# Feed-forward, first matrix: seven block products for a tile and its gate instead of eight

## The chip, the core and the metric

One core of one Trainium2 chip. The metric is the device time of one execution of the whole program in microseconds, the median of several runs. The engines are named as in the profile: PE (TensorE; PEld are its weight loads), DVE (VectorE), ACT (ScalarE), POOL (GpSimd), SP (SyncE, which here only issues transfers).

## The reference

One inference step of a decoder trunk of two layers, width 1024, for 512 prompt tokens and 8 x 4 sample tokens, 544 in all. Each layer has two half feed-forwards, one ahead of its mixers and one behind them; so the program has four feed-forward stages, and they are what the change touches:

```
x += 0.5 * gate * ((silu(a) * b) @ w_out),   a, b = split(mod(rmsnorm(x)) @ w_in, 2)
```

`w_in` is 1024 x 5632, `w_out` 2816 x 1024; `mod` multiplies by (1 + scale) and adds shift. Scale, shift and gate come from the conditioning of each sequence through a large matrix `ada_w` (adaLN); its product is cut into 36 units of 512 columns, 2 MB each, of which 32 are computed inside feed-forward stages (14, 6, 12 and 0 in the four). All is float32.

## The kernel before

The state `x` stays in SBUF, channels on partitions: 8 chunks of 128 channels by 544 tokens. A product in float32 precision is made of three in `fp32r`: each weight tile and each activation is split into a high part (an ACT copy, `split_hi`, L187) and a low part, the remainder (a DVE subtraction, `split_lo`, L192), and hi x hi, hi x lo and lo x hi are summed in PSUM. `some` (L204) issues the six matmuls of one chunk of 128 rows: three terms by two halves of 272 tokens.

A weight tile is 1024 x 128. There are two slots of raw, high and low tiles (`Weights`); SP loads a tile in three pieces (`load`, L175) as soon as the remainder of the tile that had the slot is made; ACT copies it when it has landed and the product that used the slot's high part is done; DVE makes the remainder; PE multiplies.

`ffn_stage` has 22 pairs of tiles (a tile of a and its gate tile of b) in three parts of 8, 8 and 6 pairs (`FFN_PARTS`). In each part the pairs are multiplied, then follow 8 output tiles, whose products run over the part's 8 or 6 chunks and are added to `x` by `residual` (L681 to L686). A pair is 96 matmuls: 8 chunks x 3 terms x 2 halves for `pa`, as many for `pg`. ACT applies Silu to `pa` (L748), DVE multiplies with `pg` (L790), ACT and DVE split the result into `ghi` (L752) and `glo` (L794). At the start of a stage `norm_vector` and `norm_scalar` make the normalised activations `nhi` and `nlo` chunk by chunk (L242 scales on DVE, L270 adds the shift on ACT and gives the high part, L247 the remainder), and `first_products` follows them chunk by chunk for the first pair.

Where a stage has units, one stands ahead of each pair's products: `ada_columns` (L419) and `ada_turn` (L432) on PE, `ada_copy` (L428) on ACT, `ada_add` (L441) on DVE, with two buffers for the 2 MB of a unit; `ada_load` (L410) refills them from ACT's queue.

GpSimd computes only in the HGRN2 stage (L1793, L1794). The order on every engine is written out by hand and held together by semaphores.

Of the kernel before, what the change touches and what calls it, by code (L numbers as in the profile page):

```python
# [27 lines left out]
P = 128  # L28
D, DEPTH, D_FF = 1024, 2, 2816
# [111 lines left out]
class Weights:  # L141
# [41 lines left out]
    def split_hi(self, act, where, k):  # L183
        u, slot = where
        act.wait_ge(self.raw_full[slot], 16 * PIECES * u + 16 * PIECES)
        act.wait_ge(self.mm_done, 2 * u + (slot + 1))
        act.activation(self.hi[slot][:, 0:k, :], self.raw[slot][:, 0:k, :], ACT.Copy).then_inc(self.hi_done, 1)  # L187

    def split_lo(self, dve, where, k):
        u, slot = where  # L190
        dve.wait_ge(self.hi_done, 2 * u + (slot + 1))
        dve.tensor_tensor(self.lo[slot][:, 0:k, :], self.raw[slot][:, 0:k, :],  # L192
                          self.hi[slot][:, 0:k, :].bitcast(F32), ALU.subtract).then_inc(self.lo_done, 1)
# [167 lines left out]
def trunk(nc, a, o):  # L361
    ctx = ExitStack()
    with ctx:
# [324 lines left out]
        def ffn_stage(l, which, w3, follow):  # L688

            names = NormSems.NAMES + RootSems.NAMES + AdaSems.NAMES + ("silu_done", "prod_done", "gh_done", "gl_done", "res_done", "x_done")  # L690
            with stage(nc, *names) as sems, ExitStack() as st:
                s, root, ada = NormSems(sems[0:5]), RootSems(sems[5:11]), AdaSems(sems[11:18])
                silu_done, prod_done, gh_done, gl_done, res_done, x_done = sems[18:]
                units = ADA_IN_FFN[l, which]
                if units:
                    ada_raw = [sb(f"ada_raw{i}", [P, DC, UNIT], at=st) for i in range(2)]
                    md = sb("md", [P, 2, P], at=st)
                nhi, nlo = (sb(n, [P, DC, T], F32R, at=st) for n in ("nhi", "nlo"))
                ghi, glo = (sb(n, [P, KMAX, T], F32R, at=st) for n in ("ghi", "glo"))
                tmp, ts = norm_buffers(st)  # L700
                sq = sb("sq", [P, 2, T], at=st)
                sa, g32 = sq, tmp
                rt = sb("rt", [P, 2, NSMP], at=st)
                pa = [ps(f"pa{i}", 2, st) for i in range(2)]
                pg = [ps(f"pg{i}", 2, st) for i in range(2)]
                block = st.enter_context(nc.Block())
                w_in = a["ffn_w_in"][l, which]
                w_out = a["ffn_w_out"][l, which]

                parts = []  # L710
                t = j0 = 0
                for n in FFN_PARTS:
                    after = DC if len(parts) + 1 < len(FFN_PARTS) or follow else None
                    parts.append((n, j0, t, t + 2 * n, after))
                    t, j0 = t + 2 * n + DC, j0 + n

                @block.sync
                def _(sp):
                    for n, j0, ti, to, _ in parts:
                        first = 1 if j0 == 0 else 0  # L720
                        for j in range(first, n):
                            for q in range(2):
                                c = (j + j0) * P + q * D_FF
                                wt.load(sp, wt.at(ti + q, j), wt.columns(DC, w_in[:, c:c + P]))
                            if j0 + j == 1:
                                for i in range(min(2, len(units))):
                                    ada_load(sp, ada, ada_raw, i, *units[i])
                        rows = w_out[j0 * P:(j0 + n) * P, :]
                        for c in range(DC):
                            wt.load(sp, wt.at(to + c), wt.columns(n, rows[:, c * P:(c + 1) * P]))  # L730
                    for q, tile in enumerate(follow):
                        wt.load(sp, wt.at(t + q), tile)

                @block.scalar
                def _(act):
                    norm_scalar(act, s, tmp, ts, mods, w3, nhi)
                    for n, j0, ti, to, after in parts:
                        def pair(j, last):
                            for q in range(2):
                                i = j0 + j + q - 1  # L740
                                if 0 <= i < len(units):
                                    ada_copy(act, ada, pg[q][:, 0, HALF:], md, i)
                                    if i + 2 < len(units):
                                        ada_load(act, ada, ada_raw, i + 2, *units[i + 2])
                                k = n if last and q == 1 else DC
                                wt.split_hi(act, wt.at(ti + 2 * q + 2, j), k)
                                act.wait_ge(prod_done, j + (j0 + q + 1))
                                act.activation(strided(sa[:, q, :], [HALF, 2], [1, HALF]), pa[q][:, :, 0:HALF],  # L748
                                               ACT.Silu).then_inc(silu_done, 1)
                                wt.split_hi(act, wt.at(ti + 2 * q + 3, j), k)  # L750
                                act.wait_ge(prod_done, j + (j0 + q + 3))
                                act.activation(ghi[:, bass.ds(j + q, 1), :], g32[:, q, :].unsqueeze(1), ACT.Copy).then_inc(gh_done, 1)  # L752

                        def chunks(c, last):
                            for q in range(2):
                                if not last:
                                    wt.split_hi(act, wt.at(to + q + 2, c), n)
                                elif after:
                                    wt.split_hi(act, wt.at(to + q + 2, c), after)

                        for j in range(0, n, 2):
                            pair(j, j == n - 2)
                        if j0 + n < D_FF // P:
                            for c in range(DC // 2):
                                chunks(c, c == DC // 2 - 1)
                            continue
                        for c in range(DC):
                            if c + 2 < DC or after:
                                wt.split_hi(act, wt.at(to + c + 2), n if c + 2 < DC else after)
                            act.wait_ge(res_done, DC * (len(parts) - 1) + c + 3)  # L770
                            square(act, root, x, c, sq)
# [3 lines left out]
                def _(dve):  # L775
                    dve.sem_inc(prod_done, 2)
                    dve.sem_inc(res_done, 2)
                    norm_vector(dve, s, x, rs, tmp, ts, mods, w3, nhi, nlo)
                    for c0, (n, j0, ti, to, after) in enumerate(parts):
                        def pair(j, last):  # L780
                            for q in range(2):
                                i = j0 + j + q - 2
                                if 0 <= i < len(units):
                                    ada_add(dve, ada, pg[q][:, 1, HALF:], units, i)
# [1423 lines left out]
```

## Time and profile before

| what | value |
|---|---|
| time, median of 3 runs (range) | 3281.62 us (3279.41 to 3281.9) |
| the profiled execution | 3281.45 us, span 3279.7 us |
| busy: PE, PEld, DVE, ACT, POOL | 92%, 87%, 41%, 29%, 2% of the span |
| PE instructions | 24911 |
| mean granted clock of TensorE | 0.941 |
| bytes read from HBM, written | 344.10 MB, 39.07 MB |

Rows of the profile that group instructions give line, engine, operation, output<-inputs with partitions x elements, count | busy us, mean ns of one | idle time of the engine just before them and what ended it. Rows of a timeline give start us, duration us, engine, line, operation, with the idle time before it and its releaser in brackets; "x2" merges two instructions. A start time counts from the beginning of the span.

### The profile page before, as it was taken

Reading aid. Unit: us, or ns where it says so; the run is one execution under the profiler, and the core shown is the slowest. Engines: PE = TensorE matmul, PEld = TensorE weight load, DVE = VectorE, ACT = ScalarE, POOL = GpSimd, SP = SyncE. Lnnn points to the kernel's source line nnn. Section 1 sums busy time; section 2 is a strip of 40 time slices with the busy share of each in tenths; the row PEclk is TensorE's granted clock in tenths of the full one; section 3 lists DMA queues with packets and bytes.
Section 4 is the critical chain, followed back from the end, with each engine's and each line's share of the span. In section 5 each row is a group of like instructions: output and inputs, shape, how many; then the busy total and the mean of one; then the engine's idle time right before and its main releaser. Section 6 shows DMA issues by size and latency. Waiting matters only on the chain. (4 is left out here: it accounts for less than half of the span.)

```text
span 3279.7 us, 58783 instructions
## 1 busy us (share of the span) xinstructions
PE 3015.7 (92%) x24911; PEld 2855.5 (87%) x24911; DVE 1347.5 (41%) x2793; ACT 964.3 (29%) x1594; POOL 57.4 (2%) x32
## 2 busy tenths in 40 slices
PE   6999998989679898999989999888985998899997
PEld 4999998878469898999989999887873998899997
DVE  3332334356355454333343333443553635433334
ACT  2222222344243233222232222332443413322222
POOL 0000000000030000000000000000000300000000
PEclk7999999899889899999989999989997998899998
DMA  6746224431542335332256522263215425232331
GB/s 201 248 133 205 85 81 148 99 116 53 116 123 79 112 114 194 107 90 85 83 176 202 159 84 87 88 177 99 65 51 150 100 70 158 65 90 85 91 89 62
DMA packets 523703, 378.65 MB, mean 115 GB/s; under 512 B 43058, under 2 KB 469448, under 8 KB 522131
## 3 DMA queue, kind: packets, MB, share of 16 engines
q1 hardware_dynamic: 490068, 303.10, 32.3%
q10 hardware_dynamic: 33376, 71.83, 6.4%
q8 instruction: 194, 3.18, 0.4%
q14 instruction: 65, 0.53, 0.1%
HBM read 344.10 MB, written 39.07 MB: 117 GB/s over the span
## 5 line engine op out<-in xcount | busy, mean ns | idle before, releaser
L192 DVE TENSOR_TENSOR w_lo<-w_raw,w_hi 128x1024 fp32r<-128x1024 f32 (+1 forms) x390 | 480.8, 1233 | 1096.8 <-ACT w_hi L187 1096.6
L187 ACT ACTIVATE w_hi<-w_raw 128x1024 fp32r<-128x1024 f32 (+1 forms) x390 | 405.7, 1041 | 1312.6 <-PE pa L204 681.0
L204 PE MATMUL pa<-nhi,w_hi 128*128 128x272 f32 x1408 | 297.6, 293 | 29.1 <-DVE nlo L247 27.3
L204 PE MATMUL pa<-nhi,w_lo 128*128 128x272 f32 x1408 | 293.1, 290 | 0.0
L204 PE MATMUL pa<-ghi,w_hi 128*128 128x272 f32 x1408 | 291.4, 288 | 1.3 <-DVE glo L794 1.3
L204 PE MATMUL pg<-nhi,w_lo 128*128 128x272 f32 x1408 | 292.5, 289 | 0.0
L204 PE MATMUL pa<-nlo,w_hi 128*128 128x272 f32 x1408 | 292.5, 289 | 0.0
L204 PE MATMUL pg<-nhi,w_hi 128*128 128x272 f32 x1408 | 292.3, 289 | 0.0
L204 PE MATMUL pg<-nlo,w_hi 128*128 128x272 f32 x1408 | 291.5, 289 | 0.0
L204 PE MATMUL pa<-ghi,w_lo 128*128 128x272 f32 x1408 | 291.4, 288 | 0.0
L204 PE MATMUL pa<-glo,w_hi 128*128 128x272 f32 x1408 | 290.2, 288 | 0.0
L204 PEld LDWEIGHTS pa<-nhi,w_hi 128*128 128x128 f32 x1408 | 223.5, 191 | 30.4 <-issue 29.8
L204 PE MATMUL pd<-nhi,w_hi 128*128 128x272 f32 x1024 | 226.8, 303 | 0.7 <-ACT rs L1735 0.7
L204 PEld LDWEIGHTS pa<-nlo,w_hi 128*128 128x128 f32 x1408 | 223.6, 190 | 0.0
L204 PEld LDWEIGHTS pa<-ghi,w_hi 128*128 128x128 f32 x1408 | 221.3, 188 | 2.1 <-DVE glo L794 2.1
L204 PEld LDWEIGHTS pg<-nhi,w_hi 128*128 128x128 f32 x1408 | 222.5, 189 | 0.0
L204 PEld LDWEIGHTS pg<-nlo,w_hi 128*128 128x128 f32 x1408 | 222.5, 190 | 0.0
L204 PEld LDWEIGHTS pa<-nhi,w_lo 128*128 128x128 f32 x1408 | 221.8, 190 | 0.0
L204 PEld LDWEIGHTS pa<-glo,w_hi 128*128 128x128 f32 x1408 | 221.3, 189 | 0.0
L204 PEld LDWEIGHTS pg<-nhi,w_lo 128*128 128x128 f32 x1408 | 221.0, 190 | 0.0
L204 PEld LDWEIGHTS pa<-ghi,w_lo 128*128 128x128 f32 x1408 | 219.7, 189 | 0.0
L204 PE MATMUL pd<-nlo,w_hi 128*128 128x272 f32 x1024 | 213.7, 291 | 0.0
(351 smaller groups left out, 4611.4 us busy)
## 6 DMA issues: line engine op xcount, KB each, us to landing
w_raw<-in_ffn_w_in SPq DMA_DIRECT2D x352, 192.0 KB, 2.8
ada_raw<-in_ada_w ACTq DMA_DIRECT2D x26, 2048.0 KB, 9.8
w_raw<-in_w_in SPq DMA_DIRECT2D x156, 192.0 KB, 3.0
w_raw<-in_ffn_w_out SPq DMA_DIRECT2D x128, 192.0 KB, 2.7
w_raw<-in_ffn_w_in SPq DMA_DIRECT2D x176, 128.0 KB, 2.9
ada_raw<-in_ada_w SPq DMA_DIRECT2D x10, 2048.0 KB, 15.3
w_raw<-in_ffn_w_out SPq DMA_DIRECT2D x160, 128.0 KB, 2.4
w_raw<-in_w_in SPq DMA_DIRECT2D x94, 128.0 KB, 3.1
```

What stands on the lines that cost most here:

```text
L187: act.activation(self.hi[slot][:, 0:k, :], self.raw[slot][:, 0:k, :], ACT.Copy).then_inc(self.hi_done, 1)
L192: dve.tensor_tensor(self.lo[slot][:, 0:k, :], self.raw[slot][:, 0:k, :], self.hi[slot][:, 0:k, :].bitcast(F32), ALU.subtract).then_inc(sel ...
L204: mm = pe.matmul(out[:, half, 0:HALF], w[slot][:, k0 + n, :], x[:, n, half * HALF:(half + 1) * HALF], start=(n == 0 and w is self.hi and x ...
```

## The change

The 2 x 2 x 2 block product of a pair (a tile and its gate, two halves of the 1024 rows, two halves of the tokens) is computed with seven products in place of eight, in the form with 15 additions. Each of the seven runs over 4 chunks and 272 tokens in three split terms: 12 matmuls. Three of them use half a weight tile as it is, four use sums of half tiles.

- GpSimd makes the four sums of a pair (128x512 each, `weight_sums`); ACT copies them to `shi`, DVE makes the remainders `slo`. The high and low parts of the weight tiles themselves are now made of the halves in use only (`k0`).
- At the start of a stage the seven token blocks (`bhi`, `blo`) are made: two chunks at a time, DVE scales, ACT adds the shift into `n32`, GpSimd makes the four sums of tokens (128x272, `token_sums`), ACT copies, DVE makes the remainders. PE does the first pair chunk by chunk behind them.
- Each of the seven products has a PSUM bank of its own; ACT copies the first to `uu`, DVE adds the others (seven additions) into `sa` and `g32`. The eighth bank, `pu`, is for the units.
- SP's load of a tile also waits until GpSimd has made the sums of the pair that had the slot. The unit of the adaLN product stands behind the third block product; its transfer has one buffer instead of two.
- The first output tile of a part waits for all seven additions of the last pair.

The core of the diff:

```diff
-                    ada_raw = [sb(f"ada_raw{i}", [P, DC, UNIT], at=st) for i in range(2)]
+                    ada_raw = [sb("ada_raw", [P, DC, UNIT], at=st)]
...
                 @block.sync
                 def _(sp):
+                    for t in range(2, len(loads)):
+                        if t - 2 in pair_of:
+                            sp.wait_ge(sum_done, 4 * pair_of[t - 2] + 4)
+                        wt.load(sp, wt.at(t), loads[t])
+                        if t == 3 and units:
+                            ada_load(sp, ada, ada_raw, 0, *units[0])
+
+                @block.gpsimd
+                def _(pool):
+                    def weight_sums(jj, ta):
+                        wa, wb = (wt.raw[wt.at(ta + q)[1]] for q in range(2))
+                        for q in range(2):
+                            wt.landed(pool, wt.at(ta + q))
+                        if jj >= 1:
+                            pool.wait_ge(slo_done, 4 * jj)
+                        pool.tensor_tensor(sums[:, 0, :, :], wb[:, 0:H2, :], wb[:, H2:DC, :], ALU.add).then_inc(sum_done, 1)
+                        pool.wait_ge(sum_done, 4 * jj + 1)
+                        pool.tensor_tensor(sums[:, 1, :, :], sums[:, 0, :, :], wa[:, 0:H2, :], ALU.subtract).then_inc(sum_done, 1)
+                        pool.tensor_tensor(sums[:, 2, :, :], wa[:, 0:H2, :], wb[:, 0:H2, :], ALU.subtract).then_inc(sum_done, 1)
+                        pool.wait_ge(sum_done, 4 * jj + 2)
+                        pool.tensor_tensor(sums[:, 3, :, :], wa[:, H2:DC, :], sums[:, 1, :, :], ALU.subtract).then_inc(sum_done, 1)
...
+                    weight_sums(0, 0)
+                    for c in range(H2):
+                        token_sums(c)
+                    for n, j0, ti, to in parts:
+                        for j in range(1 if j0 == 0 else 0, n):
+                            weight_sums(j0 + j, ti + 2 * j)
...
                 @block.scalar
                 def _(act):
+                    for c in range(H2):
+                        for e in range(2):
+                            act.wait_ge(xr_done, 2 * c + e + 1)
...
+                            act.activation(n32[:, c % 2, e, 0:SEQ], tmp[:, (2 * c + e) % 3, 0:SEQ], ACT.Identity,
+                                           bias=mods[:, 3 * w3, c + H2 * e, 0:1]).then_inc(n_done, 1)
...
+                        act.activation(bhi[:, 0:2, c, :], n32[:, c % 2, :, 0:HALF], ACT.Copy).then_inc(bh_done, 1)
+                        act.activation(bhi[:, 6, c, :], n32[:, c % 2, 1, HALF:T], ACT.Copy).then_inc(bh_done, 1)
+                        act.wait_ge(t_done, 4 * c + 4)
+                        act.activation(bhi[:, 2:6, c, :], tb[:, c % 2, :, :], ACT.Copy).then_inc(bh_done, 1)
+                        if c == 0:
+                            for i in range(4):
+                                sum_hi(act, 0, i)
...
                 @block.vector
                 def _(dve):
...
+                            dve.wait_ge(u1_done, jj + 1)
+                            wt.multiplied(dve, wt.at(ta))
...
+                            add(sa[:, 0, :], 2, 0)
+                            if j >= 1:
+                                save(jj - 1)
+                            lo_of(dve, ta + 2)
+                            lo_of(dve, ta + 3)
+                            if j + 1 < n:
+                                sum_lo(dve, jj + 1, 0)
...
+                            add(uu[:, 1, :], 6, 0)
+                            dve.wait_ge(ev_done, 7 * jj + 2)
+                            add(uu[:, 3, :], 5, 1)
+                            if j + 1 < n:
+                                sum_lo(dve, jj + 1, 1)
...
+                            add(uu[:, 2, :], 7, 1)
...
+                            add(g32[:, 0, :], 4, 2)
+                            add(g32[:, 1, :], 5, 2)
+                            if j + 1 < n:
+                                sum_lo(dve, jj + 1, 2)
...
+                            add(sa[:, 1, :], 3, 3)
+                            if j + 1 < n:
+                                sum_lo(dve, jj + 1, 3)
+                            dve.wait_ge(silu_done, 2 * jj + 2)
+                            dve.wait_ge(ev_done, 7 * jj + 7)
+                            dve.tensor_tensor(g32[:, :, :], sa[:, :, :], g32[:, :, :], ALU.mult).then_inc(prod_done, 1)
...
                 @block.tensor
                 def _(pe):
+                        for wp, bp in ((0, bhi), (0, blo), (1, bhi)):
+                            mm = pe.matmul(prod[i], w[wp][:, k0 + c, :], bp[:, b, c, :], start=(c == 0 and wp == 0 and bp is bhi),
+                                           stop=(c == H2 - 1 and wp == 1))
...
+                        steps = [(1, wa, 0, 0), (2, wa, H2, 1), (4, wb, H2, 2), (5, ws(0), 0, 3), (6, ws(1), 0, 4), (7, ws(2), 0, 5),
+                                 (3, ws(3), 0, 6)]
...
+                            if i == 4 and jj - 1 < len(units):
+                                if jj >= 2:
+                                    pe.wait_ge(ada.add_done, jj - 1)
+                                ada_columns(pe, ada, pu, ada_raw, jj - 1)
...
+                        done = 7 * (j0 + n)
+                        pe.wait_ge(ev_done, done)
```

## Rows read from the trace of the kernel before

**Rows 1.** The page, part 1: busy us (share of the span) x instructions.

```profile
PE 3015.7 (92%) x24911; PEld 2855.5 (87%) x24911; DVE 1347.5 (41%) x2793; ACT 964.3 (29%) x1594; POOL 57.4 (2%) x32
```

**Rows 2.** Table of windows: us, PE, PEld, DVE, ACT, POOL busy (x), PEclk, DMA, GB/s.

```profile
2985.00:3090.00 105.00, 105.00 (x840) 105.00 (x839) 32.92 (x42) 26.72 (x32) 0.00 (x0) 1.00 0.31 91
```

**Rows 3.** Timeline, first stage: a unit on PE, and two copies of weights on ACT.

```profile
93.73 1.96 PE L419 MATMUL pg<-ada_raw,cp 128*32 128x128 f32 x64
...
116.33 1.06 ACT L187 ACTIVATE w_hi<-w_raw 128x1024 fp32r<-128x1024 f32 x1 [4.52 <-PE pa L204]
...
130.66 1.06 ACT L187 ACTIVATE w_hi<-w_raw 128x1024 fp32r<-128x1024 f32 x1 [4.51 <-PE pa L204]
```

**Rows 4.** Groups of instructions by line and shape, DVE.

```profile
L192 DVE TENSOR_TENSOR w_lo<-w_raw,w_hi 128x1024 fp32r<-128x1024 f32 x358 | 450.4, 1258 | 1066.6 <-ACT w_hi L187 1066.4
L794 DVE TENSOR_TENSOR glo<-tmp,ghi 128x544 fp32r<-128x544 f32 x88 | 63.8, 725 | 63.8 <-ACT ghi L752 63.8
...
L686 DVE TENSOR_TENSOR x<-x,rt 128x32 f32<-128x32 f32 x112 | 20.3, 181 | 0.0
```

**Rows 5.** The same view, ACT.

```profile
L187 ACT ACTIVATE w_hi<-w_raw 128x1024 fp32r<-128x1024 f32 x358 | 378.6, 1058 | 1220.4 <-PE pa L204 607.5 <-PE pg L204 350.8 <-PE pp L204 146.0
L752 ACT ACTIVATE ghi<-tmp 128x544 fp32r<-128x544 f32 x88 | 58.0, 659 | 168.2 <-DVE tmp L790 168.2
...
L270 ACT ACTIVATE nhi<-tmp,mods 128x512 fp32r<-128x512 f32 x48 | 34.7, 723 | 51.9 <-DVE tmp L242 51.9
```

**Rows 6.** The same view, GpSimd.

```profile
L1793 POOL TENSOR_TENSOR f<-bc 128x1024 f32<-128x1024 f32 x6 | 11.4, 1895 | 2501.9 <-DVE bc L1818 2488.6 <-DVE pj L1830 13.3
L1794 POOL TENSOR_TENSOR pj<-bc 128x1024 f32<-128x1024 f32 x4 | 10.1, 2537 | 0.0
...
L1793 POOL TENSOR_TENSOR f<-bc 128x1088 f32<-128x1088 f32 x2 | 4.0, 2002 | 12.1 <-DVE pj L1830 12.1
```

**Rows 7.** Timeline of the HGRN2 stage, where DVE and GpSimd work side by side.

```profile
950.07 1.97 POOL L1794 TENSOR_TENSOR pj<-bc 128x1024 f32<-128x1024 f32 x1
...
950.35 2.77 DVE L1828 TENSOR_TENSOR pj<-f,pj 128x1024 f32<-128x1024 f32 x1 [5.95 <-ACT f L1757]
...
953.04 1.21 DVE L1830 TENSOR_TENSOR pj<-f,pj 128x1024 f32<-128x1024 f32 x1
954.28 2.66 DVE L1845 COPY_PREDICATED at<-level,b 128x512 f32<-128x512 uint32 x4
954.33 1.90 POOL L1793 TENSOR_TENSOR f<-bc 128x1024 f32<-128x1024 f32 x1 [2.29 <-DVE pj L1830]
...
962.23 1.28 DVE L192 TENSOR_TENSOR w_lo<-w_raw,w_hi 128x1024 fp32r<-128x1024 f32 x1 [0.30 <-ACT w_hi L187]
962.39 3.10 POOL L1794 TENSOR_TENSOR pj<-bc 128x1024 f32<-128x1024 f32 x1
```

**Rows 8.** Starts of the first and the last stage: timeline rows, and one window.

```profile
76.29 0.75 DVE L242 SCALAR_TENSOR_TENSOR tmp<-x,mods,rs 128x512 f32<-128x512 f32 x1 [2.49 <-PEq L138]
...
2840.66 0.75 DVE L242 SCALAR_TENSOR_TENSOR tmp<-x,mods,rs 128x512 f32<-128x512 f32 x1 [2.04 <-PEq L138]
...
2844.47 0.79 PE L204 MATMUL pa<-nhi,w_hi 128*128 128x272 f32 x2 [6.21 <-DVE nlo L247]
...
2860.17 0.49 PE L204 MATMUL pa<-nhi,w_hi 128*128 128x272 f32 x2 [1.82 <-DVE w_lo L192]
...
2861.70:2864.90 3.20, 3.20 (x16) 3.20 (x15) 2.48 (x3) 0.66 (x1) 0.00 (x0) 0.50 0.69 199
```

**Rows 9.** Transfers: six issues on SP, then median us to landing (three rows).

```profile
76.05 3.02 SPq L175 DMA_DIRECT2D w_raw<-in_ffn_w_in  x6
...
ada_raw<-in_ada_w ACTq DMA_DIRECT2D x6, 2048.0 KB, 10.1
...
w_raw<-in_ffn_w_in SPq DMA_DIRECT2D x12, 128.0 KB, 6.7
...
w_raw<-in_ffn_w_in SPq DMA_DIRECT2D x10, 128.0 KB, 2.9
```

More of the change, by code:

```diff
@@ L708, in ffn_stage @@
                 w_out = a["ffn_w_out"][l, which]
+                per_seq = lambda v: strided(v[:, 0, 1:NSEQ], [NSEQ, DC], [1, NB], [0, NI])
+                token = lambda v, step: strided(v, [step, DC], [NI, NB], [1, NI])
+                shift, scale = mods[:, 3 * w3, :, :], mods[:, 3 * w3 + 1, :, :]
                 parts = []
+                loads, rows_of, pair_of = [], [], {}
                 t = j0 = 0
                 for n in FFN_PARTS:
-                    after = DC if len(parts) + 1 < len(FFN_PARTS) or follow else None
@@ L714, in ffn_stage @@
-                    parts.append((n, j0, t, t + 2 * n, after))
-                    t, j0 = t + 2 * n + DC, j0 + n
+                    parts.append((n, j0, t, t + 2 * n))
+                    for j in range(n):
+                        for q in range(2):
+                            pair_of[t + 2 * j + q] = j0 + j
+                            c = (j0 + j) * P + q * D_FF
+                            loads.append(wt.columns(DC, w_in[:, c:c + P]))
+                            rows_of.append((H2 * q, DC))
@@ new lines, in ffn_stage, with hi_of, lo_of @@
+                    loads += [wt.columns(n, w_out[j0 * P:(j0 + n) * P, c * P:(c + 1) * P]) for c in range(DC)]
+                    rows_of += [(0, n)] * DC
+                    t, j0 = t + 2 * n + DC, j0 + n
+                NT = t
+                loads += follow
+                rows_of += [(0, DC)] * len(follow)
+                def hi_of(act, t):
+                    if t < len(loads):
+                        k0, k = rows_of[t]
+                        wt.split_hi(act, wt.at(t), k, k0)
+                def lo_of(dve, t):
+                    if t < len(loads):
+                        k0, k = rows_of[t]
+                        wt.split_lo(dve, wt.at(t), k, k0)
@@ L717, in _ @@
                 @block.sync
                 def _(sp):
[L719 to L730, printed above, removed]
@@ L734, in _ @@
                 @block.scalar
                 def _(act):
[L736 to L765, printed above, removed]
@@ new lines, in _ @@
+                    scaled(0)
+                    smp = token(ts[:, 0, :], NSMP)
+                    dve.tensor_tensor(smp, token(x[:, 0, SEQ:T], T), token(rs[:, SEQ:T], 0), ALU.mult).then_inc(sm_done, 1)
+                    scaled(1)
+                    dve.wait_ge(sm_done, 1)
+                    dve.tensor_tensor(smp, smp, per_seq(scale), ALU.mult).then_inc(sm_done, 1)
+                    dve.wait_ge(sm_done, 2)
+                    dve.tensor_tensor(smp, smp, per_seq(shift), ALU.add).then_inc(sm_done, 1)
@@ L852, in _ @@
+                    for c0, (n, j0, ti, to) in enumerate(parts):
+                        for j in range(n):
+                            pair(j0 + j, ti + 2 * j, c0)
+                        done = 7 * (j0 + n)
+                        pe.wait_ge(ev_done, done)
                         pe.wait_ge(gl_done, j0 + n - 2)
[L853 removed]
                         wt.product(pe, wt.at(to), pa[0], ghi, glo, n, landed=gl_done, count=j0 + n)
[L855 removed]
```

276 lines of the change are left out of this document (191 added, 85 removed).

## The prediction

> **What bounds the kernel now.** I read the page's busy shares first: PE works 92% of the span, DVE 41%, ACT 29%, GpSimd 2% [rows 1]. The stages differ, so the next view is the table of windows: in a feed-forward stretch PE is busy all the time and does 840 products in 105 us, 0.125 us each, at a granted clock of 1.00 [rows 2]. A tile and its gate are 96 of them, 12.0 us. Where a unit of the adaLN product (64 records, 1.96 us) stands between, the same two tiles take 14.33 us, from one ACT copy of weights to the same copy of the next pair [rows 3], so 2.33 us for the unit. In these stretches PE's own work sets the end; DVE and ACT wait for it. What is worth asking is whether the other engines still fit behind a shorter PE.
>
> **The change, part by part.**
>
> *PE in a pair.* Seven block products of 4 chunks x 3 split terms are 84 products where there were 96: 10.5 us for 12.0. Of the 88 pairs the first of each stage is another matter (below). 84 x 1.50 = 126 us is the most that can be won. The count follows from the code, so that the products do not become fewer is no case.
>
> *DVE in a pair.* Before: two remainders of 1024 at 1.26, a multiplication and a remainder of 544 at 0.725 [rows 4], 4.0 us. After: 15 instructions. By the line through the rows of 32 and of 544 elements (0.18 and 0.725), one of 512 takes 0.69 and one of 272 takes 0.43. Two remainders of half tiles and four of sums (6 x 0.69), one remainder and one multiplication of 544 (2 x 0.725) have both inputs in SBUF: 5.6. Seven additions read PSUM and one SBUF tile: 7 x 0.43 = 3.0. Together 8.6; one that follows another starts 0.08 before its end (953.04 after 950.35 + 2.77, [rows 7]), so 7.5 us. ACT, by its line (0.659 for 544, 1.058 for 1024 [rows 5], so 0.63 and 0.43): six copies of 512, one of 272, one of 544, two Silu of 272, 5.7 us in all, hidden.
>
> *GpSimd.* Four sums of 512 in a pair. Its rows give 1.895 for 1024 and 2.002 for 1088 [rows 6], so 1.67 ns an element: 1.04 for 512, 0.64 for 272. Bounds: 0.95 (half of 1.895) and 1.27 (half of the 2.537, which has waits in it). I take 1.04: the unhindered rows are the nearest. The Trainium skill, "GPSIMD Engine Reference", "Elementwise — side-by-side cycle accounting", gives 4497 ns for two inputs of 2048 elements, about 1.12 for 512 as an estimate; its operands are dense, while one operand of our rows repeats a column. By it the sum below would end some 18 us later; no run here shows dense operands.
>
> *The port that both use.* A DVE operation with two SBUF inputs that meets a GpSimd operation waits until that ends: 2.77 us in place of 1.21, just what the GpSimd operation had left; the other way round GpSimd takes 3.10 for 1.97. DVE operations that read PSUM beside one SBUF tile (four of 0.66 from 954.28) run beside a GpSimd operation of 1.90 that nothing lengthens [rows 7]. What happens where both always have the next operation ready, no row shows. If they take turns, a pair in which DVE is late runs so: multiplication; first sum beside the first addition; remainder, sum, remainder, sum, remainder, sum; then additions and the other remainders. One sum holds DVE up 0.7, three hold it up 1.04 each: 7.5 + 3.8 = 11.3 us; with the semaphores 11.4. Bounds: 7.5 (every sum falls where DVE waits; then PE's 10.5 decides) and 7.5 + 4 x 1.27 = 12.6.
>
> *The loads.* A tile's load now also waits until the sums of the pair before in its slot are made, and the next sums wait for that load. Queued behind it on SP are all later loads; ACT's copies and GpSimd wait for them. Round: 6.1 us from first to last sum in the order above, six issues in 3.0, and 2.9 from the last issue to landing less the 0.5 of its own slot [rows 9]: 11.5. It agrees with DVE's 11.4, and neither hides in 10.5.
>
> *Body without units.* A part's first pair finds DVE busy with four remainders of sums and the residual of the last output tile until 5.3; its last pair makes no sums, but two remainders of 1024: 5.6. A part of 8: 5.3 + 7 x 11.4 + 5.6 = 90.7 for 96.0; of 6: 67.9 for 72.0; the last stage's seven pairs, with no late start: 3.2 + 6 x 11.4 + 5.6 = 77.2 for 84.0. There are two, four and one of these: 10.6 + 16.4 + 6.8 = 34 us won. PE idles 0.9 in each pair; the gap of 1.82 in the old trace was followed by the lower clock [rows 8], so I book nothing for shorter ones, with a bound of 0.9 a pair (40 us) if they count.
>
> *Body with units.* PE needs 10.5 + 2.33 = 12.8, more than DVE's 11.4 and 0.4 for the unit. The one buffer that is left for a unit makes a round of its own: 1.96 of columns, 0.3 copy on ACT, 10.1 from issue to landing [rows 9]: 12.4, just inside; I take 12.9. Won 1.43 x 32 = 46; the five pairs beside them 0.6 each; the wait before the first output product, now for all seven evictions (one addition and its semaphore, 0.6), five times: 46 us in all. Its other bound is the loads' round with the 6.7 us that third pieces took beside a unit's transfer [rows 9]: rival 3.
>
> *The start of a stage.* Before: 17.4 us from the first scaled chunk to the end of the first pair where a unit follows (76.29 to 93.73 [rows 3, 8]); in the last stage 19.5 to the next product, then 1.2 lost at clock 0.50 (16 products in 3.2 us where 0.125 each would be 26 [rows 8]). The first product came 3.8 after the start. After, each of 4 chunk pairs passes DVE (scale), ACT (shift), GpSimd (four token sums, three of them in a chain), ACT (copy of 1088), DVE (remainder of 1088, 1.3), and ACT does not begin the next chunk before. Chunk 0: four weight sums (4.2) in turn with eight DVE operations let the token sums begin at 7.0; four of 0.64 with three waits end at 11.8; copy 1.1; remainder 1.3: PE starts at 14.3. Chunk 1: four copies of sums on ACT (2.3), shift of two chunks and samples (1.7), token sums with three waits (2.7 + 1.1), copy 1.1 and semaphores: 9.2 later. Chunks 2 and 3: the same without the copies of sums and one wait, 6.2 and 6.3. The last 21 products at the lower clock, 0.20 each: 4.2. Sum 40.2. Lost: 3 x (40.2 - 17.4) + (40.2 - 19.5 - 1.2) = 88 us. Bounds: without port waits chunk 0 is there at 9.3 and the pair ends at 31, 50 us lost; with GpSimd at its upper bound 99.
>
> **Sum.** The profiled execution took 3281.45 us (span 3279.7), 0.2 from the median 3281.62. 3281.45 - 34 - 46 + 88 = 3289 us: PE's saving is given back at the four starts and at the shared port. Its own range, with starts of 80 to 92 and port rounds of 11.1 to 11.7: 3268 to 3310.
>
> **Rivals.**
> 1. *Not slower: the turns fall into DVE's waits.* If GpSimd finds the port mostly while DVE waits for PE, a pair stays at 10.5. Decisive point: DVE and sums under 10.5 together, which needs less than 3.0 of the 4.2 us of sums to block. Then 126 won less 12 waits of 0.6 before the output products, starts 88: 3281 - 119 + 88 = 3250; with the starts unhindered too, 3213. For it: DVE's own 7.5 leaves 3 us of waiting. Against: six remainders follow each other closely.
> 2. *Slower by GpSimd.* At 1.27 for a sum, the pair takes 12.3; it passes the old 12.0 at about 1.2. Parts then win nothing, units 42, starts lose 99: 3338. For it: dense operands; against: the unhindered rows at 1.9. The skill's estimate of 1.12 lies between and gives about 3307.
> 3. *Slower by the loads beside a unit.* 6.1 + 3.0 + 6.2 = 15.3 against 12.8: over 7 pairs 17 us late, of which 8 or so are covered, because a sum is made some 7 us before its product. 8 x 5 parts = 40: 3329. For it: the 6.7 us; against: that piece met the transfer at its beginning.
>
> **How the numbers follow.** Forecast 0.42, rival 1 0.27, rival 2 0.20, rival 3 0.11. About 0.2% (6.6 us) is what a measurement of this kernel tells from no change. The forecast's own range puts 0.08 below 3275, 0.17 within, 0.17 above. Faster 0.27 + 0.08 = 0.35; same 0.17; slower 0.17 + 0.31 = 0.48. Eight times in ten: 3232 to 3340, from rival 1 with part of the better start to the whole of rival 2.
>
> **What would show it.** Right: 1056 fewer products (23855 of 24911); GpSimd busy some 460 us or more (352 sums, 64 token sums); DVE remainders of 512 with means well over 0.69; PE idle about 14 us before the first block product of a stage and several us between its chunks; PE idle about 0.9 in pairs without a unit. Wrong: pairs of 10.5 with GpSimd at work (rival 1), sums near 1.3 (rival 2), PE waiting for weights or for DVE in pairs with a unit (rival 3), or a first pair that ends near 31 us.

## The result, and the profile of the changed kernel

The changed kernel takes 3372.21 us (median of 4 runs, 3364.71 to 3379.28) against 3280.51 us for the kernel before beside it: ratio 1.0284, 95% interval 1.0271 to 1.0298. That is 92 us slower, and 83 us above the forecast, outside its range. The profiled execution took 3375.51 us (span 3373.7), at a mean granted clock of 0.923 where it was 0.941.

The page of the changed kernel, its first lines, to be laid beside [rows 1]:

```profile
span 3373.7 us, 60049 instructions
...
PE 2944.0 (87%) x23855; PEld 2769.3 (82%) x23855; DVE 1968.7 (58%) x3773; ACT 1220.9 (36%) x2182; POOL 697.7 (21%) x448
```

PE has its 1056 products fewer and is busy 72 us less, but the span is 94 us longer: PE waits where it worked before. No engine is near its full span, so what holds PE up must be a chain over several of them. GpSimd's 698 us are far above the 460 that the prediction named as its least.

The groups of instructions by line and shape, GpSimd and DVE (columns as in [rows 4]):

```profile
L784 POOL TENSOR_TENSOR sums<-sums,w_raw 128x512 f32<-128x512 f32 x88 | 151.8, 1725 | 6.9
L782 POOL TENSOR_TENSOR sums<-w_raw 128x512 f32<-128x512 f32 x88 | 133.2, 1514 | 1545.2 <-DMA w_raw<-in_ffn_w_in 901.6 <-POOLq L138 643.6
...
L196 DVE TENSOR_TENSOR w_lo<-w_raw,w_hi 128x1024 fp32r<-128x1024 f32 x274 | 360.2, 1315 | 477.0 <-ACT w_hi L191 476.7
L817 DVE TENSOR_TENSOR slo<-sums,shi 128x512 fp32r<-128x512 f32 x352 | 317.0, 909 | 12.3 <-ACT shi L813 5.4
L196 DVE TENSOR_TENSOR w_lo<-w_raw,w_hi 128x512 fp32r<-128x512 f32 x84 | 121.0, 1440 | 46.5 <-ACT w_hi L191 46.1
```

Three things are to be seen. A sum takes 1.5 to 1.7 us, not 1.04. DVE's remainders of 512 take 0.91 and 1.44, not 0.69: the shared port, as forecast. And GpSimd's idle time ahead of a pair's first sum (L782) is ended for 902 us by a load of a weight tile: GpSimd, which makes the loads late, then waits for them. The rows of w_lo also show a misreading: all of a tile of a is used (one half in each of two products), so its remainder is one of 1024; only the gate's is one of 512.

A pair without a unit, in the timeline of the last stage (columns as ahead of the prediction):

```profile
3102.70 1.72 POOL L787 TENSOR_TENSOR sums<-w_raw,sums 128x512 f32<-128x512 f32 x1
3110.53 1.63 POOL L782 TENSOR_TENSOR sums<-w_raw 128x512 f32<-128x512 f32 x1 [6.11 <-DMA w_raw<-in_ffn_w_in]
3112.23 1.61 POOL L784 TENSOR_TENSOR sums<-sums,w_raw 128x512 f32<-128x512 f32 x1
3113.82 1.73 POOL L785 TENSOR_TENSOR sums<-w_raw 128x512 f32<-128x512 f32 x1
3115.50 1.72 POOL L787 TENSOR_TENSOR sums<-w_raw,sums 128x512 f32<-128x512 f32 x1
...
3104.26 0.36 PE L993 MATMUL pa<-bhi,w_hi 128*128 128x272 f32 x1 [1.68 <-DVE g L925]
3117.06 0.36 PE L993 MATMUL pa<-bhi,w_hi 128*128 128x272 f32 x1 [1.98 <-DVE g L925]
...
3108.69 1.06 ACT L191 ACTIVATE w_hi<-w_raw 128x1024 fp32r<-128x1024 f32 x1 [1.35 <-DMA w_raw<-in_ffn_w_in]
...
3109.78 2.92 DVE L196 TENSOR_TENSOR w_lo<-w_raw,w_hi 128x1024 fp32r<-128x1024 f32 x2 [1.68 <-ACT w_hi L191]
```

What SP's loads waited for, over the whole execution (us in total, times, longest us):

```profile
SPq L175 <- POOL sums L787: 491.4, 86, 7.7
```

The last sum (L787) ends at 3104.42; the loads wait for it, and 6.11 us later both tiles are there and the next first sum begins; four sums end at 3117.22. Sums 6.69 and load 6.11 make 12.80 us, and PE goes from the first matmul of its third block product, which waits for a bank, to the same of the next pair in 3117.06 - 3104.26 = 12.80. PE's own row names DVE, but DVE waited for ACT (1.68) and ACT for the load (1.35). From one multiplication (L968) to the next, the six full pairs of that part take 12.67 to 14.03 us, where the old kernel took 12.0 [rows 2].

The start of the last stage, to be laid beside [rows 8]:

```profile
2896.28 1.26 POOL L782 TENSOR_TENSOR sums<-w_raw 128x512 f32<-128x512 f32 x1 [255.94 <-POOLq L138]
...
2912.52 0.83 POOL L795 TENSOR_TENSOR tb<-n 128x272 f32<-128x272 f32 x1 [4.67 <-ACT n L830]
...
2896.32 1.76 DVE L889 SCALAR_TENSOR_TENSOR tmp<-x,mods,rs 128x512 f32<-128x512 f32 x1 [1.95 <-PEq L138]
...
2910.37 0.59 PE L993 MATMUL pa<-bhi,w_hi 128*128 128x272 f32 x1 [16.36 <-DVE blo L898]
2919.42 0.59 PE L993 MATMUL pa<-bhi,w_hi 128*128 128x272 f32 x1 [4.85 <-DVE blo L898]
2926.16 0.39 PE L993 MATMUL pa<-bhi,w_hi 128*128 128x272 f32 x1 [2.01 <-DVE blo L898]
2932.38 0.40 PE L993 MATMUL pa<-bhi,w_hi 128*128 128x272 f32 x1 [1.80 <-DVE blo L898]
```

PE starts 14.05 us after the first scaled chunk, the others follow 9.05, 6.74 and 6.22 later, the last 21 products take 3.8: 39.9 us (40.4 in the first stage). The forecast had 14.3, 9.2, 6.2, 6.3 and 4.2, together 40.2. The scaling itself takes 1.76 for 0.75, because the first sum of weights, begun 0.04 us before, has the port.

Where the 94 us are (profiled executions). A part is taken from the first scaled chunk of a stage, or the end of the output tiles before it, to its own first output product; the starts are those of the first stage, three times, and of the last:

| stretch | forecast | measured |
|---|---|---|
| four starts | +88 | +88 |
| parts without units | -34 | +32 |
| parts with units | -46 | -37 |
| output phases (two of the twelve at a granted clock of 0.97: 49.9 us for 48.3) | 0 | +2 |
| outside the four stages | 0 | +9 |

The starts are right, the pairs with units nearly so. The miss is the pair without a unit. The last row is not shown to come from the change: over the profiles of all runs below, what lies outside the stages takes 1585 to 1598 us (1589 in the kernel before), though no edit touches it. So where totals are compared, a difference of some 10 us can come from there.

### The profile page after: what moved, and what is told of

Its sections match the earlier page's. It is cut to its first block and busy times, and to the rows that moved or that the text cites. A ratio compares the mean times of both kernels' runs of the same rounds, so it can differ in the third digit from the quotient of the medians.

```text
span 3373.7 us, 60049 instructions
## 1 busy us (share of the span) xinstructions
PE 2944.0 (87%) x23855; PEld 2769.3 (82%) x23855; DVE 1968.7 (58%) x3773; ACT 1220.9 (36%) x2182; POOL 697.7 (21%) x448
## 5 line engine op out<-in xcount | busy, mean ns | idle before, releaser
L196 DVE TENSOR_TENSOR w_lo<-w_raw,w_hi 128x1024 fp32r<-128x1024 f32 (+2 forms) x390 | 509.4, 1312 | 528.5 <-ACT w_hi L191 527.9
L191 ACT ACTIVATE w_hi<-w_raw 128x1024 fp32r<-128x1024 f32 (+2 forms) x390 | 369.5, 948 | 804.0 <-PE pa L208 401.0
L993 PE MATMUL pa<-bhi,w_hi 128*128 128x272 f32 x1056 | 321.7, 305 | 166.5 <-DVE blo L898 101.2
L782 POOL TENSOR_TENSOR sums<-w_raw 128x512 f32<-128x512 f32 x88 | 133.2, 1514 | 1545.2 <-DMA w_raw<-in_ffn_w_in 901.6
L813 ACT ACTIVATE shi<-sums 128x512 fp32r<-128x512 f32 x352 | 217.0, 629 | 296.3 <-POOL sums L787 68.3
L817 DVE TENSOR_TENSOR slo<-sums,shi 128x512 fp32r<-128x512 f32 x352 | 317.0, 909 | 12.3 <-ACT shi L813 5.4
L993 PE MATMUL pg<-bhi,shi 128*128 128x272 f32 x1056 | 317.9, 301 | 0.0
L993 PE MATMUL pa<-bhi,w_lo 128*128 128x272 f32 x1056 | 314.9, 298 | 0.0
L993 PE MATMUL pg<-bhi,slo 128*128 128x272 f32 x1056 | 313.1, 296 | 0.0
L993 PE MATMUL pg<-blo,shi 128*128 128x272 f32 x1056 | 313.1, 296 | 0.0
L993 PE MATMUL pa<-blo,w_hi 128*128 128x272 f32 x1056 | 312.9, 296 | 0.0
```

The lines of the kernel that those rows point to most:

```text
L191: act.activation(self.hi[slot][:, k0:k, :], self.raw[slot][:, k0:k, :], ACT.Copy).then_inc(self.hi_done, 1)
L196: dve.tensor_tensor(self.lo[slot][:, k0:k, :], self.raw[slot][:, k0:k, :], self.hi[slot][:, k0:k, :].bitcast(F32), ALU.subtract).then_inc( ...
L782: pool.tensor_tensor(sums[:, 0, :, :], wb[:, 0:H2, :], wb[:, H2:DC, :], ALU.add).then_inc(sum_done, 1)
L813: act.activation(shi[:, i, :, :], sums[:, i, :, :], ACT.Copy).then_inc(shi_done, 1)
L817: dve.tensor_tensor(slo[:, i, :, :], sums[:, i, :, :], shi[:, i, :, :].bitcast(F32), ALU.subtract).then_inc(slo_done, 1)
L993: mm = pe.matmul(prod[i], w[wp][:, k0 + c, :], bp[:, b, c, :], start=(c == 0 and wp == 0 and bp is bhi), stop=(c == H2 - 1 and wp == 1))
```

## The experiments

Theory A: the round of sums and load is the bound of those pairs. Theory B: DVE's own queue with its waits at the port is, and the loads are late only because DVE is. Theory C: the chain from DVE's evictions back to PE's banks is. Each kernel was timed beside the kernel before on the same chip; ratios are to that.

**Four raw buffers in the feed-forward stages.** All work stays; a load now waits for the sums and the remainder of the tile four places back, so no longer for those of the pair just before.

```diff
+                extra = [sb(f"w_extra{i}", [P, DC, P], at=st) for i in range(2)]
...
-                        if t - 2 in pair_of:
-                            sp.wait_ge(sum_done, 4 * pair_of[t - 2] + 4)
+                    if t - 4 in pair_of:
+                        sp.wait_ge(sum_done, 4 * pair_of[t - 4] + 4)
```

> The loads get four raw buffers in the feed-forward stages in place of two; the order on every engine and all sums stay. Theory A (the round of sums and load is the bound: sums 6.7 us, then the next load 6.1 us, 12.8 us per pair): the round goes, and the next bound is DVE with its waits at the port, about 11.3 us of the 12.8. 52 pairs have no unit beside them, some 45 of them with a pair behind them in the part: 45 x 1.4 = 63 us less, about 3309 us. Theory B (DVE's own queue with its waits at the port sets the pair, the loads are late only because DVE is): no change, 3367 to 3377 us. Theory C (the chain from evictions on DVE back to PE's banks): no change either.

Measured: 3313.13 us, ratio 1.0101 (1.0084 to 1.0118), 59 us less than the change: theory A. In the profiles it is 64 us: 38 in parts without units, 10 in parts with them, 3 in output phases, and 13 outside the stages, where nothing was changed. That the total came within 4 us of the 3309 expected is partly luck, since the next bound is not 11.3 us but 12.16, as this kernel's timeline shows:

```profile
3198.43 1.62 POOL L806 TENSOR_TENSOR sums<-w_extra 128x512 f32<-128x512 f32 x1 [4.87 <-DVE slo L841]
3200.13 1.67 POOL L808 TENSOR_TENSOR sums<-sums,w_extra 128x512 f32<-128x512 f32 x1
3201.76 2.26 POOL L809 TENSOR_TENSOR sums<-w_extra,w_extra 128x512 f32<-128x512 f32 x1
3203.98 1.74 POOL L811 TENSOR_TENSOR sums<-w_extra,sums 128x512 f32<-128x512 f32 x1
...
3186.02 0.72 DVE L992 TENSOR_TENSOR g<-sa,g 128x544 f32<-128x544 f32 x1
...
3198.18 0.72 DVE L992 TENSOR_TENSOR g<-sa,g 128x544 f32<-128x544 f32 x1
3199.03 0.44 DVE L949 TENSOR_TENSOR sa<-pa,uu 128x272 f32<-128x272 f32 x1
3199.62 1.02 DVE L945 TENSOR_TENSOR glo<-g,ghi 128x544 fp32r<-128x544 f32 x1 [0.15 <-ACT ghi L866]
3200.57 4.00 DVE L788 TENSOR_TENSOR w_lo<-w_extra,w_hi 128x1024 fp32r<-128x1024 f32 x2
3204.49 1.78 DVE L841 TENSOR_TENSOR slo<-sums,shi 128x512 fp32r<-128x512 f32 x1
```

A pair lasts 12.16 us (3186.02 to 3198.18), and DVE has hardly a gap in it. GpSimd now waits for DVE (4.87), not for a load. DVE's w_lo take 4.00 where 1.26 + 0.69 less an overlap of 0.08 would do, slo 1.78 for 0.69, glo 1.02 for 0.73: 3.5 us at the port, 8.6 of DVE's own. So without the round the pair is still above the old 12.0; A is right about what bound the kernel, and B names the next bound, 0.5 to 1.9 us below the pairs of the timeline above.

**Sums on 16 of 128 columns.** The cover of both theories is taken away together.

```diff
+                        nc_ = P if jj == 0 else 16
-                        pool.tensor_tensor(sums[:, 0, :, :], wb[:, 0:H2, :], wb[:, H2:DC, :], ALU.add).then_inc(sum_done, 1)
+                        pool.tensor_tensor(sums[:, 0, :, 0:nc_], wb[:, 0:H2, 0:nc_], wb[:, H2:DC, 0:nc_], ALU.add).then_inc(sum_done, 1)
...
```

> GpSimd makes the sums of every pair but a stage's first on 16 of 128 columns only; the rest of each sum is left as it was, so the output is not the reference's. ACT, DVE and PE do all their work as before. Theory A: the sums' part of the round falls from 6.7 to about 1 us, the port is nearly free, and PE's 10.5 us decide in pairs without a unit, 12.8 in pairs with one: 52 x 2.0 and a few us at the units, 3240 to 3265 us. Theory B: the port's waits go, so DVE falls to about 8 us in the pair and the time is the same as by A. Theory C (the chain of evictions): pairs stay near 12 us, above 3330 us.

Measured: 3263.70 us in one run, the kernel before 3279.14. The full pairs without a unit take 10.59 us, near the 10.5 of PE's 84 products. The chain of evictions (C) falls, and all of GpSimd's part in the body is worth some 108 us. A and B are not told apart by it.

**Fills in place of sums.** GpSimd takes as long, but reads no SBUF.

```diff
+                        if jj:
+                            for i in range(4):
+                                for z in range(2):
+                                    pool.memset(sums[:, i, :, :], 0.5).then_inc(pad_done, 1)
+                                    pool.wait_ge(pad_done, 8 * jj - 8 + 2 * i + z + 1)
+                                pool.memset(sums[:, i, :, :], 0.25).then_inc(sum_done, 1)
+                            return
```

> In place of each sum of a pair behind a stage's first GpSimd fills 128x512 three times with a constant, one after the other, so the products of the sums are not the reference's. GpSimd still takes its time in the round, but reads no SBUF. Theory A: a pair lasts as long as three fills make the round (four times three fills, and 6.1 us of load), whatever DVE's operations take; with fills of about 0.5 us that is again about 12 us and 3340 to 3370 us. Theory B (the port): DVE's remainders of 512 fall from 0.91 to about 0.69 us and the pair goes to about 10.5 to 11 us even where GpSimd's fills take the 6 us: 3260 to 3300 us.

Measured: 3374.64 us in one run. The groups of this kernel:

```profile
L785 POOL MEMSET sums<- 128x512 f32 x672 | 353.7, 526 | 921.9 <-DMA w_raw<-in_ffn_w_in 883.7 <-DVE slo L824 18.9
...
L824 DVE TENSOR_TENSOR slo<-sums,shi 128x512 fp32r<-128x512 f32 x352 | 239.3, 688 | 116.2 <-ACT shi L820 109.4
```

DVE's remainders are back at 0.688 us, DVE as a whole is busy 142 us less, and the time lies within the range of the change's four runs (3364.71 to 3379.28), a little above theory A's 3340 to 3370. Twelve fills make 6.6 us in place of sums of 6.7, the load's wait stays, and so do pairs of mostly 12.4 to 14.0. This is the clearest run, though a single one: in the changed kernel, what DVE loses at the port costs nothing by itself; the port counts only in that it stretches a sum from 1.26 to 1.7.

**Fills and four raw buffers.** With the round gone, is it the port that holds the pair at 12.16? (The expectation says 11.7, a sixth of that kernel's part of six, in which the last pair is shorter; a full pair takes 12.16.)

> Four raw buffers, and in place of the sums of pairs behind a stage's first GpSimd fills 128x512 three times for each sum (6.3 us in a pair, as seen in the run of fills with two buffers), reading no SBUF; the products of the sums are not the reference's. It asks what holds a pair at 11.7 us once the round of loads is gone. Theory P (DVE's waits at the shared port): DVE's remainders of 512 take 0.69 us again and pairs without a unit go to 10.6 us, some 45 x 1.1 = 50 us below the run with four buffers, about 3263 us. Theory Q (DVE's own work and its order, or GpSimd's time as such): pairs stay at 11.5 to 11.7 us and the time near 3310 us.

Measured: 3263.03 us in one run. Two multiplications that follow each other in its timeline, pairs of 10.59 us:

```profile
3059.09 0.72 DVE L999 TENSOR_TENSOR g<-sa,g 128x544 f32<-128x544 f32 x1
3069.68 0.72 DVE L999 TENSOR_TENSOR g<-sa,g 128x544 f32<-128x544 f32 x1
```

In its groups:

```profile
L848 DVE TENSOR_TENSOR slo<-sums,shi 128x512 fp32r<-128x512 f32 x352 | 238.8, 687 | 107.1 <-ACT shi L844 104.7
```

This is theory P. That the total was met to the microsecond is luck: a pair lost 1.57 us, not 1.1, so the parts without units are 56 us shorter, and 8 us more lie outside the stages. The order is: the round first, the port behind it, then PE.

**The gate's tile loaded first.** The round from the other side: no work and no buffer changes, SP only stops waiting for a sum that doesn't read the tile.

```diff
-                            sp.wait_ge(sum_done, 4 * pair_of[t - 2] + 4)
-                        wt.load(sp, wt.at(t), loads[t])
+                            q = t % 2
+                            behind = t + 1 - 2 * q
+                            sp.wait_ge(sum_done, 4 * pair_of[t - 2] + 3 + q)
+                        wt.load(sp, wt.at(behind), loads[behind])
```

> Two raw buffers, all sums on GpSimd, only SP's order and waits change: the gate's tile of the next pair is loaded first, as soon as three of the four sums are made (the fourth reads no gate), and then the tile of a. It takes the three issues of one tile (1.5 us) out of the round of sums and load and nothing out of any engine's work. Theory A (the round is the bound): 12.8 becomes 11.3, and DVE's turns with GpSimd at the port then hold the pair at 11.7, as with four buffers: 45 x 1.1 to 1.4 = 50 to 60 us less, 3312 to 3322 us. If ACT, which copies the tile of a first, waits for it in place of the sums, about half of that. Theory B (the round is not the bound): 3367 to 3377 us.

Measured: 3350.18 us, ratio 1.0210 (1.0190 to 1.0231), 22 us less. GpSimd in its timeline:

```profile
3115.65 1.56 POOL L785 TENSOR_TENSOR sums<-w_raw 128x512 f32<-128x512 f32 x1 [4.94 <-DMA w_raw<-in_ffn_w_in]
...
3118.91 2.27 POOL L788 TENSOR_TENSOR sums<-w_raw 128x512 f32<-128x512 f32 x1
```

The wait for the load falls from 6.11 to 4.94, 1.2 of the 1.5 us, but the sums now meet more of DVE (2.27), and nine of the last stage's 16 full pairs take 12.15 to 12.17, the port's bound, the others up to 12.9. The direction is A's. The size was missed for two reasons. I had read 11.7 as the port's bound. And the edit costs time where a part begins: from the end of the output tiles to the first multiplication behind them it takes 17.5 to 18.7 us eight times, where the change took 14.3 to 15.6, some 26 us in all. There the gate's remainder is made last, the gate's load waits for it, and the tile of a now waits behind that load:

```profile
3060.57 0.69 DVE L196 TENSOR_TENSOR w_lo<-w_raw,w_hi 128x512 fp32r<-128x512 f32 x1 [2.99 <-ACT w_hi L191]
...
3067.55 1.06 ACT L191 ACTIVATE w_hi<-w_raw 128x1024 fp32r<-128x1024 f32 x1 [4.65 <-DMA w_raw<-in_ffn_w_in]
```

SP issues the gate's load at 3061.33, as soon as that remainder is made. ACT's wait for the tile of a, which the expectation named as what would halve the gain, is seen there.

**ACT ahead at the start.** ACT shifts the next two chunks before it waits for the token sums.

```diff
+                        if c + 1 < H2:
+                            shifted(c + 1)
+                        if c == 0:
+                            for i in range(4):
+                                sum_hi(act, 0, i)
                         act.wait_ge(t_done, 4 * c + 4)
```

> At the start of a stage ACT makes the shifted tokens of the next two chunks before it waits for the four token sums of these, and the four sums of weights of the first pair are split (ACT copies, DVE remainders) ahead of the first token sums' copy and not behind it. Theory A (the chunks are late because ACT holds the next chunk back until GpSimd has answered): the first block product starts after 14 us as now, the next chunks follow after 4.5 to 5 us each (GpSimd's four token sums with their waits) instead of 9.1, 6.7 and 6.2: 7 to 8 us less at each of four starts, about 3343 us. Theory B (GpSimd and DVE hinder each other at the port and that alone sets the pace): only the copies of the sums leave the second chunk's chain, 2.5 us at each start, about 3362 us.

Measured: 3346.95 us, ratio 1.0199 (1.0182 to 1.0216), 25 us less. PE at the start of the last stage, where the first scaled chunk is at 2879.43:

```profile
2897.20 0.60 PE L1002 MATMUL pa<-bhi,w_hi 128*128 128x272 f32 x1 [20.08 <-DVE blo L906]
...
2907.12 0.40 PE L1002 MATMUL pa<-bhi,w_hi 128*128 128x272 f32 x1 [1.95 <-DVE blo L906]
2911.56 0.39 PE L1002 MATMUL pa<-bhi,w_hi 128*128 128x272 f32 x1 [1.53 <-DVE blo L906]
```

The last chunk is begun after 32.1 us where it was 36.1. The first comes later than in the change (17.8, not the 14 expected), because four slo now stand ahead of it on DVE; the rest follow at 4.4 to 5 us, which is theory A's pace. So a start gains 4.0 us and not 7 to 8, and the four first parts of the stages 17.6 us together; the rest of the 25 lies in stretches that the edit doesn't touch.

**Sums on DVE.** All pairs but the first of a part.

```diff
-                        for j in range(1 if j0 == 0 else 0, n):
-                            weight_sums(j0 + j, ti + 2 * j)
+                        if j0:
+                            weight_sums(j0, ti)
...
                             if j + 1 < n:
-                                sum_lo(dve, jj + 1, 0)
+                                weight_sum(jj + 1, ta + 2, 0)
+                                weight_sum(jj + 1, ta + 2, 1)
```

> The sums of weights of all pairs but the first of each part go from GpSimd to DVE, between its other operations; two raw buffers as in the change. Theory A (the round, made long by GpSimd's 1.7 us a sum, is the bound): a sum takes about 0.69 us on DVE, the four with what lies between them about 5 us, the round 11, and DVE's own work is 19 operations, 10.4 to 10.9 us: pairs without a unit 10.9 to 11.2 us for 12.8, 45 x 1.7 = 77 us less, about 3295 us. Theory B (DVE's work is what counts, and the sums on GpSimd were a relief): pairs stay above 12 us, 3350 us or more.

Measured: 3312.42 us, ratio 1.0092 (1.0077 to 1.0108). DVE does four operations more in each pair (0.68 to 0.69 each) and the kernel is 60 us faster than the change, where 77 were expected: theory A. Most pairs without a unit take 11.42 us, DVE's own queue, a little over the 10.9 to 11.2 expected. What the port is worth shows against the 12.16 with four buffers: there a sum on GpSimd costs DVE about 0.9 us (3.5 over four), more than making it.

**Combinations.** The first three are made of the edits above; the fourth has one more, at the start of a stage, shown against the third.

> Both earlier edits in one kernel: four raw buffers, and the start in which ACT works ahead. They touch different stretches, so their gains should add: 3313 less 25, about 3288 us. If the second pair of a stage needs what the shorter start no longer covers, less: 3295 to 3305 us.

Measured: 3301.08 us, 1.0063 (1.0047 to 1.0078): 12 us less than with four buffers alone, where 25 were expected.

> The sums of weights on DVE and the start in which ACT works ahead, two raw buffers. Theory A: 3295 less 25, about 3270 us, which is below the kernel before. Theory B: 3325 us or more.

Measured: 3299.44 us, 1.0057 (1.0043 to 1.0071): 13 us less than with DVE's sums alone. The gain of the start is not lost, though: in the profiles the four first parts of the stages are 16.3 and 15.6 us shorter, nearly the 17.6 of that edit by itself. The 25 us held more than the start, and totals differ by what lies outside the stages.

> As the one before, with four raw buffers. If with DVE's sums the round of loads is still the bound (theory A by a smaller round), pairs go from 11 to DVE's or PE's 10.6 and the time falls another 15 to 20 us, to about 3253 us; if DVE's own queue already is the bound, nothing changes (3265 to 3275 us).

Measured: 3285.99 us, 1.0024 (1.0013 to 1.0034): four buffers are still worth 13 us with DVE's sums, so some pairs met the shorter round too (up to 13.0 us with two buffers, 11.42 with four). All three are slower than their first expectations (3288, 3270 and 3253 us), which took the 25 us in full and, with DVE's sums, pairs of 11 us. The first lies in the range of its second case, but not by that case's cause: the second pair of a stage is no longer than without the shorter start (12.2 us in both).

> As the kernel with the sums on DVE, four raw buffers and ACT working ahead, but at the start of a stage DVE makes the first pair's sums of weights too, ahead of the first remainder of token sums, so that GpSimd begins with the token sums some 2.5 us after the start in place of 7. If GpSimd's work in a row (four sums of weights, then 16 of tokens) sets the length of the start, each start gets 4 us shorter: 3286 less 16, about 3270 us, below the kernel before. If DVE has become the bound of the start, its 2.8 us more eat that up: 3283 to 3290 us.

```diff
-                    weight_sums(0, 0)
...
                         low_a(c)
                         if c == 0:
+                            for i in range(4):
+                                weight_sum(0, 0, i)
                         low_b(c)
```

Measured: 3281.00 us, 1.0002 (0.9993 to 1.0011), 5 us less where 16 were expected, and in the profiles the four first parts are only 3.4 us shorter. GpSimd in its timeline, first scaled chunk at 2834.39:

```profile
2837.30 0.91 POOL L819 TENSOR_TENSOR tb<-n 128x272 f32<-128x272 f32 x1 [259.14 <-ACT n L853]
...
2852.00 1.29 POOL L819 TENSOR_TENSOR tb<-n 128x272 f32<-128x272 f32 x1 [5.81 <-ACT n L853]
```

The token sums begin after 2.9 us, not 7, but GpSimd then waits 5.81 for ACT's next shift, which waits for DVE, busy with the sums of weights: most of what one engine gained the other held back.

**The output tile begun early.** The part of the change that lets the first output product wait for all seven additions is narrowed to the bank that it writes.

```diff
-                        pe.wait_ge(ev_done, done)
+                        pe.wait_ge(ev_done, done - 6)
...
+                            else:
+                                pe.wait_ge(ev_done, done)
                             wt.product(pe, wt.at(to + c), pa[c % 2], ghi, glo, n)
```

> As the kernel with all sums of weights on DVE, four raw buffers and ACT working ahead, but the first output tile of a part waits only for the first of the last pair's seven additions (the bank that it writes), the second tile for all seven. The waits before the twelve first output products (0.5, 1.1 and 1.8 us, four each) are then hidden by 36 to 42 products of that tile: 13 us less, about 3268 us, below the kernel before. If the last pair's Silu, multiplication and split, for which that tile's last chunk waits, are late enough to be waited for there, nothing is won: 3278 to 3283 us.

Measured: 3258.05 us (3257.49 to 3261.82) against 3275.37: ratio 0.9949 (0.9936 to 0.9963), faster than the kernel before by 0.5%, and by the two ratios 17 us less than the run it builds on, where 13 were expected. In the profiles the parts are 13.9 us shorter, as expected, and the output phases 3.9, because the three that took 49.8 to 49.9 us now take 48.3. The first lines of its page:

```profile
span 3256.7 us, 60039 instructions
...
PE 2906.8 (89%) x23855; PEld 2739.6 (84%) x23855; DVE 1998.1 (61%) x4093; ACT 1210.7 (37%) x2182; POOL 177.9 (5%) x128
```

A part of eight pairs without units takes 88.0 us with its wait, for 96.0 before; a start still takes 33 us (2820.77 to 2853.9 in the last stage), 12 to 16 more than before.

## Why the prediction was wrong

*The products, the ACT copies, the starts:* right. There are 23855 products; a start takes 39.9 to 40.4 us for 40.2. *The pairs with units* won 37 us for 46; four raw buffers take 10 us off these parts, so the round reached them too.

*"Round: 6.1 us from first to last sum in the order above, six issues in 3.0, and 2.9 from the last issue to landing less the 0.5 of its own slot [rows 9]: 11.5."* This is the step that failed: the round is a bound, as it says, but both of its terms were too short. In the part of the timeline above they are 6.4 to 7.0 us of sums and 6.0 to 7.1 of load, 12.6 to 13.8 together. In the round shown, the six issues took the 3.0 us of the forecast; the next first sum began 3.6 us after the start of the last issue, where 2.9 were counted. It was also set beside DVE's 11.4 as its equal; with four buffers (59 us less) and with fills (nothing, although DVE was relieved) the two come apart, and the round alone decides in the change. With the 13.1 us that the pairs take on average in place of 11.4, the forecast's own sum would for 45 pairs be 3289 + 77 = 3366.

*"I take 1.04: the unhindered rows are the nearest."* An unhindered sum takes 1.26 (2896.28 above). The line through rows of 1024 and 1088 elements, of which one operand repeats a column, did not carry to 512 with two dense ones; the upper bound of 1.27, set aside, was the value. The port then makes 1.5 to 1.7 of it. The Trainium skill, "GPSIMD Engine Reference", "Elementwise — side-by-side cycle accounting", would have given 1.12 as an estimate: nearer than my line, and still short of the trace.

*The port.* The turns were right: 3.8 us of waits forecast in a pair, 3.5 measured with four buffers, and none with fills. The Trainium skill, "SBUF — State Buffer", "SBUF: two separate sides", says that a DVE operation with two SBUF inputs is blocked only against a GpSimd operation that reads SBUF; the fills agree (0.688 against 0.909). DVE's own work was 8.6, not 7.5: 0.57 of the difference is the remainder of a's tile, which I took for a half, and 0.35 are short gaps. Hence 12.16 for 11.4, so that rival 2's 12.3 was nearly the price of the pair without the round.

*The rivals.* Rival 1 (pairs of 10.5) is what is left when neither the round nor the port holds the pair (10.59 with fills and four buffers); a free port alone leaves it at 12.4 to 14.0 for the most part (fills and two buffers). Rival 2 had the right duration of a sum and would have given 3338. It fell short for the same reason as the forecast: neither let the longer sums lengthen the loads' round. Rival 3 looked for late loads beside the units; four buffers took 10 us off the parts with units and 38 off those without, so most of the lateness was in the pairs without one. Rival 3's own terms (17 less 8, five times) make 45, not 40.

## What to carry to other kernels

Where a buffer is freed by the slowest engine and the next work of that engine needs the refilled buffer, add its time and the transfer's: the sum is a bound of its own, however idle each of them looks. A sum put on GpSimd need not relieve DVE where DVE's operations beside it read two SBUF tiles: here DVE made the sums itself for less. Price an operation by a row of its own kind of operands, and take the upper bound where the rows differ in kind.

## What the hardware showed that was not expected

A GpSimd sum of 512 elements with two dense operands takes 1.26 us, a fill of the same size 0.526, and fills leave DVE's two-input operations at 0.688. In turns with DVE a sum takes 1.6 to 2.3, so both sides pay for each meeting at the port.
